# Two changes to a one-core decoder block: the first input tile loaded and transposed in column halves, and five convolution products moved to later steps

## The reference

```python
h = rmsnorm(x, g_mix)
proj = h @ w_in                     # 1024 x 4608: u (GLU), q, k, v, two gates
o = attention(q, k, v)              # 8 heads of 64, causal, one block of 256
z = a * sigmoid(g)                  # a, g: the halves of u + b_glu
z = causal_depthwise_conv(z, w_dw)  # 31 taps, 512 channels
cz = silu(layernorm(z + b_dw))
merged = gate_a * (o @ w_attn_up) + gate_c * (cz @ w_conv_pw + b_conv_pw)
x = x + merged @ w_out
x = x + square(relu(rmsnorm(x, g_ffn) @ w_ff1)) @ w_ff2
return rmsnorm(x, g_final)
```

## Time and profile before

| | |
|---|---|
| median of 3 runs | 353.61 us (353.55 to 353.9) |
| the profiled execution, its own time | 354.28 us |
| its span, first to last instruction | 352.5 us |
| mean granted TensorE clock | 0.999 |
| busy: PE, PEld, DVE, ACT | 98%, 82%, 71%, 54% |

### The profile page before, as it was taken

One profiled execution on the slowest core, in us unless ns is written; L12 is line 12 of the kernel. 1 busy time (PEld: TensorE's weight loads), 2 busy tenths in 40 slices (PEclk: granted clock), 3 DMA queues, 4 the chain that ended last, 5 costly groups with the idle time before them and its releaser, 6 DMA issues.

```text
span 352.5 us, 4587 instructions
## 1 busy us (share of the span) xinstructions
PE 346.4 (98%) x1727; PEld 287.3 (82%) x1727; DVE 251.2 (71%) x310; ACT 191.6 (54%) x237; POOL 3.5 (1%) x13
## 2 busy tenths in 40 slices
PE   8999999999999999999999999999999999999994
PEld 5888888787878888888888888888888888888884
DVE  2969999999889999956756836639366394563813
ACT  3985654688796458434764535525355163551534
POOL 1000000000000000000000000000000000000000
PEclk9999999999999999999999999999999999999999
DMA  8999455435353365783647481944729538260003
GB/s 283 348 387 375 160 188 185 172 123 159 123 194 120 121 238 169 249 263 102 222 129 238 155 253 72 336 140 137 253 86 286 190 124 245 107 238 0 0 0 120
DMA packets 34430, 64.24 MB, mean 182 GB/s; under 512 B 1360, under 2 KB 6000, under 8 KB 34416
## 3 DMA queue, kind: packets, MB, share of 16 engines
q1 hardware_dynamic: 34112, 63.57, 53.7%
q10 hardware_dynamic: 304, 0.48, 0.4%
HBM read 63.00 MB, written 1.05 MB: 182 GB/s over the span
## 4 chain that ended last, share of the span: by engine, by line
PE 98%; DVE 0%; issue 0%; DVEq 0%; ACT 0%
PE ps L949 21%; PE ps L951 20%; PE ps L950 20%; PE ps L1187 17%; PE ps L1189 9%; PE ps L936 4%; PE ps L995 2%; PE ps L1006 1%; PE ps L1049 1%; PE ps L1074 1%; PE ps L976 1%; PE ps L1149 0%; PE ps L1234 0%; PE ps L1233 0%; PE ps L1232 0%
## 5 line engine op out<-in xcount | busy, mean ns | idle before, releaser
L949 PE MATMUL ps<-w_hi,a_lo 128*128 128x512 f32 x272 | 107.5, 395 | 0.0
L951 PE MATMUL ps<-w_lo,a_hi 128*128 128x512 f32 x272 | 106.1, 390 | 0.0
L950 PE MATMUL ps<-w_hi,a_hi 128*128 128x512 f32 x272 | 106.0, 390 | 0.0
L1187 PE MATMUL ps<-b_both,w_hi 128*128 128x512 f32 x256 | 90.8, 399 | 0.0
L1189 PE MATMUL ps<-b_both,w_lo 128*128 128x256 f32 x256 | 71.9, 281 | 0.0
L877 DVE TENSOR_TENSOR w_lo<-raw,w_hi 128x2048 fp32r<-128x2048 f32 x28 | 63.5, 2287 | 6.4 <-ACT w_hi L609 6.4
L399 ACT CAST w_hi<-raw 128x2048 fp32r<-128x2048 f32 (+1 forms) x30 | 53.8, 1800 | 16.8 <-PE ps L951 16.8
L660 DVE TENSOR_TENSOR w_lo<-raw,w_hi 128x2048 fp32r<-128x2048 f32 x26 | 59.3, 2283 | 3.4 <-ACT w_hi L399 3.3
L949 PEld LDWEIGHTS ps<-w_hi,a_lo 128*128 128x128 f32 x272 | 51.1, 188 | 10.9 <-issue 0.3
L951 PEld LDWEIGHTS ps<-w_lo,a_hi 128*128 128x128 f32 x272 | 51.1, 188 | 11.0
L950 PEld LDWEIGHTS ps<-w_hi,a_hi 128*128 128x128 f32 x272 | 51.1, 188 | 10.0
(11 more groups left out here) (131 smaller groups left out, 258.6 us busy)
## 6 DMA issues: line engine op xcount, KB each, us to landing
raw<-in_w_ff_dram SPq DMA_DIRECT2D x32, 1024.0 KB, 5.5
raw<-in_w_in_dram SPq DMA_DIRECT2D x14, 1024.0 KB, 5.6
raw<-in_w_out_dram SPq DMA_DIRECT2D x4, 1024.0 KB, 5.0
raw<-in_w_in_dram SPq DMA_DIRECT2D x14, 256.0 KB, 5.0
raw<-in_w_attn_up_dram SPq DMA_DIRECT2D x2, 1024.0 KB, 5.0
raw<-in_w_conv_pw_dram SPq DMA_DIRECT2D x2, 1024.0 KB, 5.0
res<-in_x_dram SPq DMA_DIRECT2D x2, 512.0 KB, 3.8
raw<-in_w_in_dram SPq DMA_DIRECT2D x4, 128.0 KB, 4.0
```

What stands on the lines that cost most here:

```text
L949: nc.tensor.matmul(dst, lo[:, tok], w_hi[:, slot, k], start=start, stop=False, skip_group_check=seeded)
L950: nc.tensor.matmul(dst, hi[:, tok], w_hi[:, slot, k], start=False, stop=False, skip_group_check=seeded)
L951: return nc.tensor.matmul(dst, hi[:, tok], w_lo[:, slot, k], start=False, stop=stop, skip_group_check=seeded)
L1187: nc.tensor.matmul(ps[:, TB + c], w_hi[:, slot, k, cols], b_both[:, kk].rearrange("p a t -> p (a t)"), start=kk == 0, stop=False)
```

## The change

The load of tile 0 is cut into two loads of 512 columns with a semaphore each; tile 1's load is whole, with a new semaphore. PE transposes four chunks of tile 0 per half, then multiplies zeros of 256 columns once, then waits for tile 1. The zero products ahead are five, not seven. ACT's first square waits for both halves. In `CONV_AT` steps 7 and 8 have one product less each and step 13 three less; step 11 has two more and step 12 three more.

```diff
-WARM = 7
+WARM = 5
-CONV_AT = {2: 6, 3: 12, 4: 9, 5: 9, 6: 9, 7: 9, 8: 8, 9: 5, 10: 8, 11: 8, 12: 8, 13: 14, 14: 10, 15: 5}
+CONV_AT = {2: 6, 3: 12, 4: 9, 5: 9, 6: 9, 7: 8, 8: 7, 9: 5, 10: 8, 11: 10, 12: 11, 13: 11, 14: 10, 15: 5}
-        x_full = [sem(f"x_full{t}") for t in range(TT)]
+        x_half = [sem(f"x_half{part}") for part in range(2)]
+        x_second = sem("x_second")
-            for t in range(TT):
-                sp.dma_start(res[:, t], x_v[:, t]).then_inc(x_full[t], 16)
+            for part in range(2):
+                cols = slice(part * W, part * W + W)
+                sp.dma_start(res[:, 0, cols], x_v[:, 0, cols]).then_inc(x_half[part], 16)
+            sp.dma_start(res[:, 1], x_v[:, 1]).then_inc(x_second, 16)
-            act.wait_ge(x_full[0], 16)
+            act.wait_ge(x_half[0], 16)
+            act.wait_ge(x_half[1], 16)
             square_input(0)
             high(2)
-            act.wait_ge(x_full[1], 16)
+            act.wait_ge(x_second, 16)
             square_input(1)
-            for t in range(TT):
-                pe.wait_ge(x_full[t], 16)
-                for k in range(KD):
-                    last = transpose(x_chunk(k)[:, t * P:t * P + P], res[:, t, k * P:k * P + P])
-                    if t == TT - 1 and k % 2 == 1:
-                        last.then_inc(x_tr, 1)
+            for part in range(2):
+                pe.wait_ge(x_half[part], 16)
+                for k in range(HK * part, HK * part + HK):
+                    transpose(x_chunk(k)[:, 0:P], res[:, 0, k * P:k * P + P])
+            nc.tensor.matmul(ps[:, 0, 0:T], zero_b[:, 0:P], zero_b[:, 0:T], start=True, stop=True)
+            pe.wait_ge(x_second, 16)
+            for k in range(KD):
+                last = transpose(x_chunk(k)[:, P:T], res[:, 1, k * P:k * P + P])
+                if k % 2 == 1:
+                    last.then_inc(x_tr, 1)
```

## The result

| | before | changed |
|---|---|---|
| median | 353.89 us | 355.00 us |
| lowest and highest of 8 | 353.53 to 354.34 | 354.53 to 356.43 |
| the profiled execution, its time and span | 354.28, 352.5 | 354.72, 352.9 |

The ratio is 1.0042, with an interval from 1.0032 to 1.0053: the changed kernel is 0.4% slower. This ratio is near that of the means (355.37 and 353.89 us); the medians differ by 1.11 us, 0.3%. The forecast was 353.0 us, 0.17% faster. The highest execution of the changed kernel is 1.9 us above its lowest, where before that was 0.8 us.

The account below looks back on a forecast made before the run. PE, busy 346.4 of 352.5 us, was taken as the bound, so its start counts. An earlier start (0.37 us) and fewer stalls sum to 0.6 us: 353.61 less 0.6 is 353.0 us, range 352.5 to 354.0.

Parts of the forecast that it names:

- the landing of tile 1: Second tile of `x` at the start: it lands at 5.4 to 5.5 us, its transpositions starting at about 5.55.
- Part 1: The kernel's start: first real product at 7.1 us, third slice's at 9.95 where 10.53 stood; gain 0.6 us.
- the third issue: SP's extra load issue at the start: 0 to 0.1 us of later landing, upper bound 0.43 us.
- the shorter rows: Loads of tile 0's halves: 2 KB rows for 4 KB ones cost nothing up to 0.1 us.
- The second half of tile 0: Second of the two cut loads at the start: lands near 4.05 us, in time for its transpositions.
- Rival B: Start bound by something that stays, a late tile 1 or an early clock: 353.2 to 353.7 us, chance 0.25.
- rival A: PE's clock rises later at the start, after fewer zero products: 354.3 or 356.1 us, chance 0.1.
- the earlier start: PE at the start: tile 1's transpositions end at 7.0, first real product at 7.1, 0.37 us earlier.
- the stalls: PE's waits for `a_lo` among the first products vanish, as `a_lo` is ready when asked; 0.32 us of stalls before.
- Part 2: Convolution products moved among steps 7 to 13: gives nothing by itself; step 13's margin stays above 1 us.
- DVE's idle times: DVE in steps 11 and 12: 0.4 to 0.6 us left ahead of the fourth maxima, nearly none ahead of `w_lo`.
- rival D: DVE becomes late at step 11 or 12 and PE waits, taking the gain back: 353.6 us, chance 0.05.

Follow-up runs that it names:

- Cut_only: Kernel before with only tile 0's load cut into two column halves, PE and ACT waiting for both: 354.63 against 353.90 us, ratio 1.0021.
- after_again: The changed kernel itself, measured and traced once more: 354.92 against 353.97 us, ratio 1.0055.
- look2: One more trace of the changed kernel as it is: 354.90 us.
- look1: One more trace of the changed kernel as it is: 356.28 us.
- look3: One more trace of the changed kernel as it is: 356.41 us.
- zeros5: Kernel before with five zero products instead of seven, nothing else: 354.61 against 353.90 us, ratio 1.0017.
- conv_only: Kernel before with the five moved convolution products alone: 353.96 against 353.97 us, ratio 1.000.
- whole_load: Changed kernel with one load for tile 0, five zero products kept, ACT's wait for the second half dropped: 354.51 against 353.97 us, ratio 1.0025.
- zeros6: Kernel before with six zero products instead of seven: 353.66 against 353.83 us, ratio 0.9998.
- cut_act: Kernel before with tile 0 in two column halves and tile 1's load issued by ACT ahead of `g_mix`: 356.12 against 353.83 us, ratio 1.0063.
- cut_rows: Kernel before with tile 0 in two loads of 64 tokens, PE and ACT waiting for both: 355.80 against 353.90 us, ratio 1.0048.

## Why the prediction was wrong

**The term that failed** is the landing of tile 1 in Part 1. I priced the third issue at 0 to 0.1 us, with the whole 0.43 as the upper bound, and the shorter rows at 0 to 0.1. Tile 1 landed 1.0 to 1.9 us later than at 5.4: 0.47 us of that is its later issue (1.66 for 1.19), and the rest is that it then took 4.8 to 5.7 us for 4.2. The second half of tile 0, put at 4.05, landed at 4.3 to 5.0. The argument was that the DMA engines are full from 3 us on and that 1 KB rows move at the same rate. That rate is of a queue in full flow; it doesn't bound what a cut does to the first loads, and the bound from one row, which showed no such load, was too narrow. Cut_only puts this term at 0.7 us of time. Rival B had tile 1 late by the issue alone; the longer time from issue to landing stood in no rival.

**The chance that failed** is rival A's, 0.1. In 10 of 22 executions of the changed kernel the time was 355.9 us or more. Of the five traces of it, the three of executions below 355 (the first one, after_again, look2) have tile 1 at 2.4 GHz, while look1 and look3 reach that level near 10.7 us. The two prices of A (354.3 and 356.1) enclose what zeros5's trace (355.3) shows, and the changed kernel, with both losses, went to 357.9. The place was right (short transpositions with idle time around them); I gave it a small chance since the one trace had risen at 6.7. A single trace can't give a chance for something that differs between executions.

**The two losses together.** In the medians each costs 0.7 us alone and both together 1.0 to 1.1. That doesn't say that one hides part of the other, for a median hardly shows how far a high third or half of the executions lies above the rest. In the means cut_only costs 0.75 us and zeros5 0.71, 1.5 together, and the changed kernel cost 1.5 us in the first measurement and 1.8 in after_again. The means fit a plain sum.

**The gain wasn't there either.** I took 0.37 us for the earlier start, and 0.2 for the stalls, from a profiled execution that was itself among the longer ones: 354.28 us, with a late enough clock that tile 0 hid the landing of tile 1. In the profiled execution of conv_only, 353.48 us, with PE's program as before, the clock is up during tile 0:

```profile
4.49 2.21 PE L936 MATMUL ps<-ident,res 128*128 128x128 f32 x16
6.53 0.38 PE L990 MATMUL ps<-zero_b 128*128 128x512 bf16 x1
6.78 0.70 PE L995 MATMUL ps<-w_hi,a_hi 128*128 128x512 f32 x2
```

It takes 2.21 us for what took 3.02, and the first product comes at 6.78, bound by the landing of tile 1. There an earlier start of tile 0 gains nothing, as rival B said ("the gain goes to 0"), and whole_load and zeros6 agree: PE starts tile 0 at 3.99 and 4.30, and neither is faster than before. The forecast should have been made against an execution near the median. Of the 2.0 us between forecast and result the gain that wasn't there is 0.6 and the loss 1.1; the other 0.3 us is that the median of the kernel before, 353.61 in three executions, came out at 353.89 in eight.

**What held.** PE is never late again behind the start; the shift of 0.38 us is carried unchanged to the end. The zero product count moves PE to 3.44 and 3.64 as forecast (3.4 and 3.6), the first half lands at 3.4 (3.35). Part 2 is worth nothing and costs nothing (conv_only). DVE's idle times ahead of the fourth maxima (0.49) and of `w_lo` in step 12 (0.18) are as forecast, and rival D is out. The stall on `a_lo` was said to vanish; it didn't, since ACT and PE came late together (0.24 us of waiting at 8.48).

The Trainium skill (DMA: Bandwidth & Descriptors, Bandwidth) asks for large transfers. The kernel with the smaller loads was slower here, by 0.7 us in cut_only, against my reading of it. But the trace doesn't show the reason to be a lower rate of small loads: from 2.5 to 3.5 us, mostly halves, DMA moved 352 GB/s in the changed kernel and 331 in cut_only, near the page's 341 for 1 MB, which is for loads issued from GpSimd. What the page on TensorE says of transpositions (the Trainium skill, TensorE: Matmul & The Clock Gate, Part 4) doesn't hold in its strict form here. In cut_act PE did nothing but transpositions from 5.42 us on, and the last 512-column zero product ahead of them started at 3.73. The weight loads of these transpositions took 230 ns up to the last one at 8.9, and the clock was up right behind them, as the pace of the first products shows (0.65 us from pair to pair, not 1.21):

```profile
3.73 0.63 PE L978 MATMUL ps<-zero_b 128*128 128x512 bf16 x1
5.42 0.24 PE L938 MATMUL ps<-ident,o_t 8*128 8x8 f32 x1 [1.05 <-DMA o_t<-in_g_mix_dram]
5.90 3.52 PE L938 MATMUL ps<-ident,res 128*128 128x128 f32 x16 [0.24 <-DMA res<-in_x_dram]
9.25 0.38 PE L992 MATMUL ps<-zero_b 128*128 128x512 bf16 x1
9.28 0.81 PE L997 MATMUL ps<-w_hi,a_hi 128*128 128x512 f32 x2
9.93 0.40 PE L997 MATMUL ps<-w_hi,a_lo 128*128 128x512 f32 x1
```

## What to carry to other kernels

A transfer that the first work waits for should be divided only after a trace of the divided form: what a smaller load gives at its own landing (4.05 us became 3.4) the next load may pay more than once over (1.0 to 1.9 us later here). Filler work ahead of the first real work isn't idle time to be trimmed: with two zero products less, a third of the executions were 1.3 us longer, and the trace of one shows a late clock. Where a start depends on a state that differs between executions, take several traces before pricing it, and read the spread of the times as a measurement.

## What was not expected

- With three or four loads of x in one queue, column halves among them, DMA moved 156 to 279 GB/s from 3.5 to 4.5 us in ten traces, against 377 to 414 GB/s in the eight with two whole loads and 410 in one where the third load was in another queue. A whole tile behind two halves took 4.8 to 5.7 us to land, where 4.1 to 4.5 is usual.
- The rise of TensorE's clock from 1.2 to 2.4 GHz differs between executions of one program by more than 3.5 us (before 6.96 us in look2, whose tile 1 runs at 0.11 us a transposition, near 10.7 in look1), and the column of the granted clock read 1.00 in both; weight-load durations showed it. Where PE had no idle time it differed too: with the same PE program the weight loads take 141 ns from 4.48 us on in conv_only and only from 6.8 on in the trace of before.
- Half a tile's partitions (64) loaded at once came no sooner than the whole, in the one trace of it: the first 256 KB of cut_rows landed at 4.4 us, the whole 512 KB tile at 4.05.
